# Gates of the last mixer: one 512-column product for both activation parts, halves added on VectorE, Silu in place

## The reference, cut to what matters

```python
def gla_mixer(h, w_in, gk_up, gk_bias, o_norm, w_out):
    ...
    proj = hp @ w_in
    ...
    q, k, v, g_out, lr_f, lr_b = jnp.split(proj, [s1, s2, s3, s4, s5], axis=-1)
    ...
    o = rmsnorm_2(o, o_norm).reshape(B, L, GLA_VALUE_DIM)
    return (o * jax.nn.silu(g_out[:, pad:])) @ w_out
```

## Time and profile before

| | |
|---|---|
| Time, median of 3 runs | 2173.33 us (2171.96 to 2173.66) |
| The profiled execution's own time | 2171.96 us |
| Its span, first to last instruction | 2170.2 us |
| PE busy | 2145.3 us, 99% of the span |
| DVE busy | 1520.9 us, 70% |
| ACT busy | 1183.3 us, 55% |
| POOL busy | 220.4 us, 10% |
| Mean granted TensorE clock | 0.999 of full speed |

### The profile page before, as it was taken

One profiled execution on the slowest core, in us unless ns is written; L12 is line 12 of the kernel. 1 busy time (PEld: TensorE's weight loads), 2 busy tenths in 40 slices (PEclk: granted clock), 3 DMA queues, 4 the chain that ended last, 5 costly groups with the idle time before them and its releaser, 6 DMA issues.

```text
span 2170.2 us, 38987 instructions
## 1 busy us (share of the span) xinstructions
PE 2145.3 (99%) x14559; PEld 1986.0 (92%) x14559; DVE 1520.9 (70%) x2091; ACT 1183.3 (55%) x1781; POOL 220.4 (10%) x146
## 2 busy tenths in 40 slices
PE   9999999999999999999999999999999999999998
PEld 8888899999889999999988889999999999999987
DVE  6676765568578888888855556999777565567755
ACT  5455654545455545555544446555655565676553
POOL 0000000000003223232300000221000000012110
PEclk9999999999999999999999999999999999999999
DMA  8645566657656575666666665666345647554454
GB/s 290 216 150 158 161 202 206 200 172 238 210 156 206 182 220 188 209 197 190 215 202 203 202 203 172 189 190 196 119 120 181 184 140 234 174 157 146 137 202 157
DMA packets 259012, 405.60 MB, mean 187 GB/s; under 512 B 16671, under 2 KB 115868, under 8 KB 257852
## 3 DMA queue, kind: packets, MB, share of 16 engines
q1 hardware_dynamic: 257204, 396.87, 58.6%
q10 hardware_dynamic: 1688, 7.07, 0.9%
HBM read 396.32 MB, written 4.22 MB: 185 GB/s over the span
## 4 chain that ended last, share of the span: by engine, by line
PE 91%; DVE 5%; ACT 3%; issue 1%; DMA 0%; DVEq 0%; ACTq 0%; SPq 0%
PE bank L2319 30%; PE bank L2315 24%; PE bank L2428 14%; PE bank L2312 12%; PE bank L2912 3%; PE bank L2334 2%; DVE wboth L1396 1%; PE bank L2659 1%; ACT wboth L709 1%; PE bank L2881 1%; PE bank L2837 1%; DVE xtok L1550 1%; PE bank L2631 1%; PE bank L2697 0%; DMA xtok<-in_x 0%
## 5 line engine op out<-in xcount | busy, mean ns | idle before, releaser
L1396 DVE TENSOR_TENSOR wboth<-raw,wboth 128x1024 fp32r<-128x1024 f32 (+1 forms) x748 | 909.3, 1229 | 512.1 <-ACT wboth L709 509.4
L709 ACT ACTIVATE wboth<-raw 128x1024 fp32r<-128x1024 f32 (+1 forms) x748 | 770.6, 1039 | 604.9 <-PE bank L2315 263.4
L2315 PE MATMUL bank<-aboth,wboth 128*128 128x512 f32 x2496 | 812.6, 382 | 2.3 <-DVE aboth L1615 1.1
L2312 PE MATMUL bank<-aboth,wboth 128*128 128x256 f32 x2496 | 658.6, 274 | 1.0 <-DVE wboth L1396 1.0
L2319 PE MATMUL bank<-aboth,wboth 128*128 128x272 f32 (+1 forms) x5184 | 624.1, 280 | 4.6 <-DVE aboth L1615 3.1
L2319 PEld LDWEIGHTS bank<-aboth,wboth 128*128 128x128 f32 x5184 | 606.1, 190 | 8.5 <-issue 3.9
L2315 PEld LDWEIGHTS bank<-aboth,wboth 128*128 128x128 f32 x2496 | 461.1, 189 | 60.5 <-issue 1.5
L2312 PEld LDWEIGHTS bank<-aboth,wboth 128*128 128x128 f32 x2496 | 478.2, 192 | 12.7 <-issue 2.7
L2428 PE MATMUL bank<-wboth,ghi 128*128 128x512 f32 x704 | 209.8, 379 | 0.9 <-DVE wboth L1396 0.9
L2940 POOL CAST ghi<-pr 128x256 f32 x44 | 84.3, 1917 | 691.2 <-DVE pr L1884 691.2
L2428 PEld LDWEIGHTS bank<-wboth,ghi 128*128 128x128 f32 x704 | 133.1, 189 | 20.1 <-DVE wboth L1396 1.3
(11 more groups left out here) (373 smaller groups left out, 1870.3 us busy)
## 6 DMA issues: line engine op xcount, KB each, us to landing
raw<-in_w_up SPq DMA_DIRECT2D x176, 512.0 KB, 4.7
raw<-in_w_in SPq DMA_DIRECT2D x156, 512.0 KB, 4.4
raw<-in_attn_w_in SPq DMA_DIRECT2D x96, 512.0 KB, 4.1
raw<-in_gla_w_in SPq DMA_DIRECT2D x96, 512.0 KB, 4.0
raw<-in_w_down SPq DMA_DIRECT2D x80, 512.0 KB, 4.6
raw<-in_w_out SPq DMA_DIRECT2D x32, 512.0 KB, 4.7
raw<-in_attn_w_out SPq DMA_DIRECT2D x32, 512.0 KB, 4.2
raw<-in_gla_w_out SPq DMA_DIRECT2D x32, 512.0 KB, 4.2
```

Source lines behind the costliest of these rows:

```text
L709: act.activation(whi[:, u % RING, 0:c], raw[:, u % RAW, 0:c], ACT.Copy).then_inc(whi_ready, 1)
L1396: dve.tensor_tensor(wlo[:, u % RING, 0:c], raw[:, u % RAW, 0:c], whi[:, u % RING, 0:c].bitcast(F32), ALU.subtract).then_inc(wlo_ready, 1)
L2312: mm = pe.matmul(bank[:, base + t, 0:T], w[1][:, k, col:col + P], in_turns(rhs(0, k0 + k)), start=False, stop=False)
L2315: mm = pe.matmul(bank[:, base + t, 0:2 * T], w[0][:, k, col:col + P], parts_in_turns(both(k0 + k)), start=first, stop=last)
```

## The change

In the stage `gg`, and nowhere else, three things change.

- TensorE: `features` is called with `both=model_parts`. Each contraction tile of each output tile takes two matmuls (512 and 256 moving columns) where it took three of 256.
- VectorE: ahead of the eighth unit's split in each trip, four `tensor_reduce` instructions add the halves of banks 0 to 3 into `gg`, each waiting for its tile of the eighth unit, and each raises `acc_free`. That count released the banks from ScalarE before.
- ScalarE: the four Silu reads of PSUM (128 x 256 each) become one Silu of 128 x 1024, in place in `gg`, which waits for all four counts. It raises `g_made` (a new name of the semaphore `g_tanh`), for which the product on VectorE now waits.

```diff
+            def gates_out(i, chunk, u, n):
+
+                act.wait_ge(acc_free, 4 * (C0["gg"] + i + 1))
+                gates = gg[:, 4 * i:4 * i + 4, :]
+                act.activation(gates, gates, ACT.Silu).then_inc(g_made, 1)
+
             for i in range(TRIPS["gg"]):
-                trip("gg", i, feature_out(gg, TB, ACT.Silu), after=gla)
+                trip("gg", i, gates_out, after=gla)
...
                         dve.wait_ge(o3_scaled, 4 * h + 4)
-                        dve.wait_ge(acc_free, 4 * (C0["gg"] + h + 1))
+                        dve.wait_ge(g_made, 4 * TRIPS["ag"] + h + 1)
                         z = gg[:, 4 * h:4 * h + 4, :]
...
+            def before_gg(i, j):
+
+                squares_added(i, j)
+                if j == UNITS["gg"] - 1:
+                    for t in range(4):
+                        dve.wait_ge(tile_pass, 4 * (U0["gg"] + 8 * i + j) + t + 1)
+                        dve.tensor_reduce(halves(gg[:, 4 * i + t, :]), parts_together(bank[:, t, :]), AX.X, ALU.add).then_inc(acc_free, 1)
+
             for i in range(TRIPS["gg"]):
-                trip("gg", i, before=squares_added, after=gla)
+                trip("gg", i, before=before_gg, after=gla)
...
-                    features("gg", i, j, model(TB), TB)
+                    features("gg", i, j, model(TB), TB, both=model_parts)
```

More of the change, by code:

```diff
@@ L416, in two_blocks_kernel @@
         v_low, pT_low, scm_low, up_hi, up_lo = map(sem, "v_low pT_low scm_low up_hi up_lo".split())
-        g_tanh = sem("g_tanh")
+        g_made = sem("g_made")
         s_ready, s_biased, max_ready, max_sink, p_ready, sink_ready, sum_sink, inv_sum, p_second, p_scaled, \
@@ L1181, in tanh_out @@
                     passed(u, t + 1, i, n)
-                    act.activation(halves(gs2[:, 4 * i + t, :]), untwined(bank[:, t, 0:T2]), ACT.Tanh, scale=0.5).then_inc(g_tanh, 1)
+                    act.activation(halves(gs2[:, 4 * i + t, :]), untwined(bank[:, t, 0:T2]), ACT.Tanh, scale=0.5).then_inc(g_made, 1)
             for i in range(TRIPS["ag"]):
@@ L2008, in doubled_silu @@
                 for t in range(4):
-                    dve.wait_ge(g_tanh, 4 * i + t + 1)
+                    dve.wait_ge(g_made, 4 * i + t + 1)
                     tile = halves(gs2[:, 4 * i + t, :])
```

## The result

| | before | changed |
|---|---|---|
| Time, median (lowest to highest), 6 runs each | 2172.07 us (2171.9 to 2173.66) | 2184.47 us (2182.19 to 2185.98) |
| Profiled execution, and its span | 2171.96, 2170.2 us | 2185.98, 2184.2 us |
| Ratio, with its 95% interval | | 1.0053 (1.0043 to 1.0063) |

The change makes the kernel slower by 12.4 us between the medians, or 0.57%; the ratio in the table is that of the means. The forecast was 2182.1 us, with a range of 2176.5 to 2187.

A forecast was written before the change was run, and what follows sets the result against it. The prediction took TensorE (PE), busy 99% of the span, to bound the kernel. Its terms, -3.3 saving + 9.4 stalls + 2.7 hand-over = +8.8 us on 2171.96, plus 1.4 to the median, gave 2182.1 us, range 2176.5 to 2187.

The forecast's parts named there:

- The saving: TensorE in gg: 12.8 ns a pair, 0.10 us a unit, 3.3 us over 256 pairs, ends 3 and 3.5.
- The stall at the boundaries: Three boundaries between gg trips: PE waits 3.1 us each for VectorE to free bank 0, 9.4 us in all.
- The hand-over into `gout`: From gg's last trip to gout: late Silu, high parts, low part and splits; fifth unit 2.4 us later, counted as 2.7.
- The sum: Whole kernel: -3.3 + 9.4 + 2.7 = +8.8 us, bounds +6.3 to +10.8.
- The clock: Rival, chance 0.16: granted clock falls at the boundary stalls, adding 1.3 to 4 us; 2183.4 to 2186.1, middle 2184.7.
- my own signs: In the changed profile: PE idle about 3 us at three places, reduces behind far keys, granted clock 1.00 throughout.
- the forecast's case: Whole kernel: the forecast without any rival, 2182.1 us, own range 2179.6 to 2184.1, chance 0.62.
- the wider range: Whole kernel, 8 in 10: 2176.5 to 2187 us, taking in parts of the clock and partly covered cases and run spread.
- price per event: At each boundary stall in the clock rival: 3 us at half pace loses 1.3 us.
- The argument against it: Against the clock rival: matmuls run up to the stall's edge and right behind it, unlike at the program's end.
- The other rivals: Stalls partly covered (0.12, middle 2175.8); no stall at all (0.05, 2171); change doesn't save (0.05, 2184.8).
- Cover: Behind the reduces in gg: split, product and Silu lose nothing; VectorE's extra 2.5 us a trip fits its idle time.

The follow-up runs named there:

- e2: Changed kernel, but ScalarE reads only 256 of each bank's 512 columns with Silu and frees it; no reduces, halves not added: 2171.03 us, ratio 0.9995.
- f1: Changed kernel with 12 small unused matmuls on PE at each boundary between trips, to keep it busy: 2181.89 us, ratio 1.0043.
- e4: Changed kernel with ScalarE making the high parts of heads 1 and 2 ahead of the last Silu: 2189.35 us, ratio 1.0079.
- f2: Changed kernel with VectorE's four reduces first at each boundary, then the next head's queries, split and far keys: 2176.53 us, ratio 1.0021.
- g1: f2 with GpSimd starting its first low part only when VectorE's last product is done: 2173.97 us, ratio 1.0009.
- e1: Changed kernel with queries and far keys of heads 1 to 3 made three units earlier on VectorE: 2180.84 us, ratio 1.0043.
- h2: Kernel before, with ScalarE's split of gout's fourth unit ahead of head 3's high part and the table load: 2171.54 us, ratio 0.9996.
- f3: f2 with the last trip of gg in the old form, products and read-out: 2171.56 us, ratio 0.9997.
- h1: f3 with ScalarE's split of gout's fourth unit ahead of head 3's high part and the table load: 2170.87 us, ratio 0.9994.

## Why the prediction was right, point by point

- **The saving** was sized wrongly: 3.3 us taken, 1.6 us in the trips of e2, below my lower end of 3. The step that failed is the one that set 340.6 ns for three matmuls against 327.8 for a pair. The first comes from a stretch of the earlier trace rows with the start-up of four units in it, the second from the middle of a run. Read over the same stretch, 10.91 us before and 10.67 in e2, the difference is 7.5 ns a pair, and from the middle of both, 335 against 327.5, it is 7.5 as well; over a whole trip it is 6.4.
- **The stall at the boundaries** was right in cause, place and almost in size. The reduces started right behind the far keys, took 0.68 us for the first and 2.48 for four, and handed over after 0.15 us. The forecast stall of 3.1 us shows as 2.53 + 0.41 = 2.94 us in two trips (of f1, without the clock's share) and 2.57 + 0.36 = 2.93 in the third (e2 takes 31.07 us there instead of 31.43), of which the profile prints 2.70 as the wait. What I added to it for PE's earlier arrival, 0.4 us from four cheaper units, was too much by about half, since they were cheaper by half of that. That VectorE doesn't move was right: the reduces start at 1986.35, 0.35 us before the 1986.70 of the earlier trace rows, but the whole execution is 0.42 us ahead there; counted from the mark they start after 10.39 us, where the split started after 10.32.
- **The hand-over into `gout`** was right: 2.4 us later at the fifth unit forecast, 2.2 measured; 1.3 us for GpSimd's low part forecast, 1.06 measured; splits behind it, 0.50 and 0.47 us. The cause I gave there, splits and low parts passing one after the other, fits: a low part takes 3.36 us in the changed kernel (at 2099.05) where the first took 2.52. e4, f2 and g1 show the same between GpSimd and VectorE's last product, which I had not counted among them.
- **The sum** was +8.8 us. Without the clock's share it came to -0.42 + 2.53 + 2.53 + 2.57 + 2.20 = 9.4 us, with the trips of f1 in the place of the two disturbed by the clock. The 0.6 us between the two are mostly the saving: in the three trips 0.41 us each instead of 24 units x 0.10 / 3 = 0.8, which is 1.2 us more, the 0.5 us of saving ahead of the first mark show as 0.42, and against that stand 0.5 us less of stall and 0.2 less at the hand-over. The sum is closer than its largest error, since errors offset each other; that is luck.
- **The clock** was my first rival, at 0.16, and it came true in the median run. By my own signs, which had the clock at 1.00 through all of it, the forecast's case failed: the median lies above its range of 2179.6 to 2184.1, and the wider range holds it because this rival was counted in. Two of the six runs kept the clock at 0.999 in the mean and took 2182.19 and 2182.76 us, close to the forecast of 2182.1; three took 2184.45 to 2184.55 and the profiled one 2185.98. The rival's middle, 2184.7, is closer to the median of 2184.47 than the forecast. A part of that closeness is luck. I counted from 2173.33 us, the median of three runs; with six runs the kernel before has 2172.07. Counted from there my sum gives 2180.9, the two runs that kept their clock are 10.1 and 10.7 us slower instead of 8.8, and the median run 12.4. Its price per event was too low: 1.3 us taken from the start of the program, for 3 us at half pace, against 3.0 and 1.7 us here, where half pace lasted 6.1 and 3.4 us of work. The argument against it, that matmuls run up to the stall's edge, didn't hold, and it should have had about even odds.
- **The other rivals** fell. The reduces weren't there as the tiles came through, the stalls weren't partly covered, and the saving was smaller than taken but not as small as 0.6 us.
- **Cover.** Nothing queued behind the reduces was late at the three boundaries: PE's waits there name only L2247. The Silu of 1.06 us and VectorE's four reduces lay beside other work, as said.

## What to carry to other kernels

A cheaper product is worth only what its read-out leaves: before moving a read-out to another engine, look at what stands ahead of it in that engine's order at the moment the bank is wanted, and put the instruction that frees the bank first. Compare two forms over the same stretch, edges included, and not one form's stretch with the other's mid-run pace. Count the clock in for any new wait of some us, and check on the trace whether a VectorE instruction with both inputs in SBUF and one of GpSimd fall on the same moment: making one wait for the other can be the faster order.

## What the runs showed of the hardware that I had not expected

- The granted clock doesn't follow from the length of the wait alone. It fell to 1.2 GHz at a wait of 1.99 us (e1) and at two of 2.70 us, and stayed at 2.4 GHz behind two others of 2.00 us in e1, a third of 2.70 us and f2's of 3.78 us: seven matmuls of 512 columns in 1.78 us there, against three in 1.65 us behind e4's wait of 4.86 us. What decides between them stays open; I didn't try to settle it.
- The same wait in the same code can cost the clock in one execution and not in the next. In a stage that no edit touches PE waits 1.10 us for VectorE, at about 1759.6. In the profiled executions of f2 and h2 the granted clock is 0.74 and 0.75 from 1760 to 1762 and 0.50 from 1762 to 1764; in that of the kernel before it is 1.00 in both windows. h2's profiled run took 2172.22 us, its seven runs with a mean clock of 0.999 took 2171.23 to 2171.86. Falls of this kind are the likely reason for the two groups of times, about 1 us apart, that the kernel before, e2, f3, h1 and h2 show.
- GpSimd's work can stretch a VectorE instruction beside it to nearly three times its time: 1.23 us became 3.40 (f2), two query instructions of 1.29 us together became 3.44 (e1). In f2 that is still less than the product and the low part one after the other, 1.23 + 2.54 us.
- One matmul less of three with the same columns is worth 6.4 to 7.5 ns at full clock here, 2% of the 327.8 ns of a pair.
